# Norms of a decoder step: variance, root and reciprocal taken for five columns, and two tiles centred from PSUM

## What is computed

```python
sh, sc, g = mods[:, :, 0], mods[:, :, 1], mods[:, :, 2]
f = _swiglu(x * (1.0 + sc) + sh, w_ffn_in[l, 0], w_ffn_out[l, 0])
x = _layernorm(DEEPNORM_ALPHA * x + 0.5 * g * f, ln_g[l, 0], ln_b[l, 0])

def _layernorm(x, g, b):
    mu = jnp.mean(x, axis=-1, keepdims=True)
    var = jnp.mean(jnp.square(x - mu), axis=-1, keepdims=True)
    return (x - mu) * lax.rsqrt(var + LN_EPS) * g + b
```

## Time and profile before

| | us |
|---|---|
| median of three runs | 2399.42 |
| the three runs | 2395.73, 2399.42, 2406.4 |
| the profiled execution's own time | 2399.58 |
| its span, first to last instruction | 2397.8 |
| PE busy | 2275.1 (95%) |
| ACT, DVE, POOL busy | 726.8, 846.7, 904.9 |
| mean granted clock of TensorE | 0.968 of full |

### The profile page before, as it was taken

The page is one execution under the profiler, slowest core; times in us unless marked ns, Lnnn a source line. Parts: engine busy times, 40 slices in busy tenths (PEclk is TensorE's granted clock), DMA queues, the critical chain, the costliest instruction groups (busy, mean ns, idle before and its releaser), DMA issues.

```text
span 2397.8 us, 44766 instructions
## 1 busy us (share of the span) xinstructions
PE 2275.1 (95%) x18650; PEld 2127.4 (89%) x18650; DVE 846.7 (35%) x1001; ACT 726.8 (30%) x1049; POOL 904.9 (38%) x473
## 2 busy tenths in 40 slices
PE   7999999989998798999999999999999989999996
PEld 5999988869984388999999899998889979999995
DVE  1222213226768554222124422212343463222133
ACT  4222222252234325222222522222242225222223
POOL 2344432334420235444434444432344444444442
PEclk8999999989999998999999999999999989999998
DMA  9232376626746421323553232366623322233331
GB/s 309 81 95 87 97 236 190 207 87 195 217 130 197 143 86 55 95 87 95 188 174 98 62 96 88 89 203 195 208 89 96 89 72 71 87 94 90 103 88 48
DMA packets 455586, 300.60 MB, mean 125 GB/s; under 512 B 20446, under 2 KB 435006, under 8 KB 455350
## 3 DMA queue, kind: packets, MB, share of 16 engines
q1 hardware_dynamic: 455478, 299.04, 41.0%
HBM read 293.45 MB, written 5.55 MB: 125 GB/s over the span
## 4 chain that ended last, share of the span: by engine, by line
PE 80%; issue 7%; DVE 4%; POOL 4%; SPq 2%; ACT 1%; DMA 1%; POOLq 0%; DVEq 0%; ACTq 0%
PE ps L822 71%; PE ps L845 2%; POOL x L490 2%; POOL w_lo L759 2%; PE ps L884 1%; DVE sq L1833 1%; PE ps L835 1%; SPq L556 1%; SPq L551 1%; POOL samp_t L503 1%; DMA ada_w<-w_ada 1%; PE ps L898 1%; DVE x L1813 1%; DMA ada_first<-w_ada 0%; DVE h_lo L1799 0%
## 5 line engine op out<-in xcount | busy, mean ns | idle before, releaser
L759 POOL TENSOR_TENSOR w_lo<-raw,w_hi 128x1024 fp32r<-128x1024 f32 (+1 forms) x303 | 791.7, 2613 | 1230.5 <-ACT w_hi L1441 1230.3
L822 PE MATMUL ps<-h_hi,w_hi 128*128 128x260 f32 x3584 | 726.7, 284 | 15.1 <-DVE h_lo L2102 8.9
L822 PE MATMUL ps<-h_hi,w_lo 128*128 128x260 f32 x3584 | 724.5, 284 | 0.0
L822 PE MATMUL ps<-h_lo,w_hi 128*128 128x260 f32 x3584 | 723.7, 284 | 0.0
L1441 ACT ACTIVATE w_hi<-raw 128x1024 fp32r<-128x1024 f32 (+1 forms) x303 | 341.3, 1127 | 1159.4 <-PE ps L822 1089.6
L822 PEld LDWEIGHTS ps<-h_hi,w_hi 128*128 128x128 f32 x3584 | 555.3, 189 | 22.1 <-DVE h_lo L2102 9.3
L822 PEld LDWEIGHTS ps<-h_hi,w_lo 128*128 128x128 f32 x3584 | 555.1, 189 | 0.0
L822 PEld LDWEIGHTS ps<-h_lo,w_hi 128*128 128x128 f32 x3584 | 553.7, 189 | 0.0
L822 PE MATMUL ps<-hid_hi,w_hi 128*128 128x260 f32 x1408 | 294.5, 290 | 0.0
L2169 DVE TENSOR_TENSOR gated<-silu_a,ps 128x520 f32<-128x520 f32 x88 | 61.3, 697 | 656.8 <-PE ps L822 638.2
L822 PE MATMUL ps<-hid_hi,w_lo 128*128 128x260 f32 x1408 | 283.9, 283 | 0.0
(11 more groups left out here) (294 smaller groups left out, 1719.1 us busy)
## 6 DMA issues: line engine op xcount, KB each, us to landing
raw<-w_ffn_in SPq DMA_DIRECT2D x173, 512.0 KB, 3.6
ada_w<-w_ada SPq DMA_DIRECT2D x120, 512.0 KB, 6.3
raw<-w_ffn_out SPq DMA_DIRECT2D x64, 704.0 KB, 4.5
pages<-cache_k SPq DMA_DIRECT2D x64, 256.0 KB, 3.3
pages<-cache_v SPq DMA_DIRECT2D x64, 256.0 KB, 3.4
raw<-w_in_even SPq DMA_DIRECT2D x27, 512.0 KB, 5.3
raw<-w_in_odd SPq DMA_DIRECT2D x23, 512.0 KB, 3.6
ada_first<-w_ada SPq DMA_DIRECT2D x10, 1024.0 KB, 11.9
```

The costliest lines, as they stand in the source:

```text
L759: pool.tensor_tensor(w_lo[:, k, 0:kt, :], raw[:, k, 0:kt, :], w_hi[:, k, 0:kt, :].bitcast(F32), ALU.subtract).then_inc(chunk_cut, chunks)
L822: mm = pe.matmul(ps[:, 2 * q + half, 0:HT], w[:, k, t, :], v[:, kt0 + t, half, :], start=start and t == 0 and step == 0, stop=stop and t = ...
```

## The change

PE no longer makes the variance as a 128x520 tile. `column_sums` uses 128 tokens of the sums of squares as the weights and one column of `mean_w` as the moving operand; the result is one column with the tokens along the partitions. Four blocks of 128 tokens and a fifth that ends with the last token (overlapping the fourth) make five columns for the mean square, from two parts each, and five for the difference of mean and `shift`: 15 matmuls. ACT squares five columns, DVE subtracts, ACT takes the root, DVE the reciprocal, all on 128x5. Then each column is multiplied into the identity, which gives diagonal blocks (three on DVE, two on ACT, the last of them eight columns wide), and two matmuls with a block of ones spread the values over all partitions, into `pair(2)`, from which DVE normalises as before.

DVE centres two tiles, and takes the mean from PSUM for them; POOL centres the others. In the norms with conditioning groups, PE does one group, then waits for the blocks and spreads them, then does the other three; ACT stores the sums of all four groups behind its own blocks.

```diff
-CENTRE = 1
+CENTRE = 2
+TOKENS_AT = (0, 128, 256, 384, NTOK - 128)
...
-            eng.tensor_tensor(x[:, t], x[:, t], mean[:, :, :], ALU.subtract).then_inc(centred[part], 1)
+            eng.tensor_tensor(x[:, t], x[:, t], mean[:, :, :] if part else pair(2), ALU.subtract).then_inc(centred[part], 1)
...
+            def column_sums(bank, *parts):
+
+                for j, at in enumerate(TOKENS_AT):
+                    for v in parts:
+                        mm = pe.matmul(ps[:, bank, j:j + 1], v.rearrange("p h c -> p (h c)")[:, at:at + 128], mean_w[:, 0:1],
+                                       start=v is parts[0], stop=v is parts[-1])
+                return mm
+
+            def spread_rdev(n):
+
+                pe.wait_ge(spread_made, len(TOKENS_AT) * (n + 1))
+                for half in range(2):
+                    mm = pe.matmul(ps[:, 4 + half, 0:HT], ones, spread[:, half, :], start=True, stop=True)
+                mm.then_inc(rdev_done, 1)
...
-                pe.wait_ge(sq_added, (KT - 2) * (n + 1))
-                for half in range(2):
-                    pe.matmul(ps[:, half, 0:HT], mean_w, sq_sum[:, half, :], start=True, stop=False)
                 pe.wait_ge(samp_added, KT * (n + 1))
...
                 pe.wait_ge(squared, KT * (n + 1))
-                for half in range(2):
-                    mm = pe.matmul(ps[:, half, 0:HT], mean_w, sq[:, (KT - 1) % 2, half, :], start=False, stop=True)
-                mm.then_inc(var_done, 1)
+                pe.wait_ge(sq_added, (KT - 2) * (n + 1))
+                column_sums(1, sq_sum[:, :, :], sq[:, (KT - 1) % 2])
+                pe.wait_ge(delta_steps, 5 * n + 1)
+                column_sums(0, shift[:, :, :]).then_inc(var_done, 1)
                 for i in after:
                     group(n, i)
                     if i > after[0]:
                         turn_group(n, i - 1)
+                    else:
+                        spread_rdev(n)
+                if not after:
+                    spread_rdev(n)
...
-                act.wait_ge(delta_steps, 3 * n + 1)
-                act.activation(shift[:, :, :], shift[:, :, :], ACT.Square).then_inc(delta_steps, 1)
-                if ADAS[n]:
-                    group_sums(n, after_groups(n)[0])
-                act.wait_ge(delta_steps, 3 * n + 3)
+                act.wait_ge(var_done, n + 1)
+                act.activation(delta_sq, ps[:, 0, 0:5], ACT.Square, scale=D / 128).then_inc(delta_steps, 1)
+                act.wait_ge(delta_steps, 5 * n + 3)
                 act.wait_ge(eps_ready, 2)
-                act.activation(dev, dev, ACT.Sqrt, bias=eps_ln[:, :]).then_inc(dev_done, 1)
-                for i in after_groups(n)[1:]:
+                act.activation(dev, dev, ACT.Sqrt, bias=eps_ln[:, :]).then_inc(delta_steps, 1)
+                act.wait_ge(delta_steps, 5 * n + 5)
+                for j, at, of in ((3, 384, ident), (4, 512, ident[:, 120:128])):
+                    act.activation(spread_flat[:, at:at + of.shape[1]], of, ACT.Identity, scale=rdev[:, j:j + 1]).then_inc(spread_made, 1)
+                for i in after_groups(n):
                     group_sums(n, i)
...
                 dve.tensor_tensor(shift[:, :, :], pair(2), shift[:, :, :], ALU.subtract).then_inc(delta_steps, 1)
-                dve.wait_ge(delta_steps, d0 + 2)
-                dve.wait_ge(var_done, n + 1)
-                dve.tensor_tensor(dev, pair(0), shift[:, :, :], ALU.subtract).then_inc(delta_steps, 1)
                 centre(dve, n, 0)
-                dve.wait_ge(dev_done, n + 1)
-                dve.reciprocal(pair(2), dev).then_inc(rdev_done, 1)
+                dve.wait_ge(delta_steps, 5 * n + 2)
+                dve.tensor_tensor(dev, ps[:, 1, 0:5], delta_sq, ALU.subtract).then_inc(delta_steps, 1)
+                dve.wait_ge(delta_steps, 5 * n + 4)
+                dve.reciprocal(rdev, dev).then_inc(delta_steps, 1)
+                dve.wait_ge(delta_steps, 5 * n + 5)
+                for j in range(3):
+                    dve.tensor_scalar(spread_flat[:, 128 * j:128 * j + 128], ident, rdev[:, j:j + 1], None, ALU.mult
+                                      ).then_inc(spread_made, 1)
                 dve.wait_ge(rdev_done, n + 1)
```

More of the change, by code:

```diff
@@ L225, in build_step @@
         sq = put("sq", [128, 2, 2, HT], F32, R_TMP + 12 * NTOK)
-        dev = sq[:, 0]
+        spread = sq[:, 0]
+        spread_flat = spread.rearrange("p h c -> p (h c)")
+        norm_cols = put("norm_cols", [128, 3, 8], F32, R_TMP + 4 * NTOK)
+        delta_sq, dev, rdev = (norm_cols[:, u, 0:5] for u in range(3))
         res = new("res", [128, 1710])
@@ L369, in build_step @@
         var_done = sem("var_done")
-        dev_done = sem("dev_done")
+        spread_made = sem("spread_made")
         rdev_done = sem("rdev_done")
@@ L1862, in norm @@
             def norm(n):
-                d0 = 3 * n
                 dve.wait_ge(mean_ready, n + 1)
                 dve.tensor_tensor(shift[:, :, :], pair(2), shift[:, :, :], ALU.subtract).then_inc(delta_steps, 1)
-                dve.wait_ge(delta_steps, d0 + 2)
-                dve.wait_ge(var_done, n + 1)
-                dve.tensor_tensor(dev, pair(0), shift[:, :, :], ALU.subtract).then_inc(delta_steps, 1)
                 centre(dve, n, 0)
-                dve.wait_ge(dev_done, n + 1)
-                dve.reciprocal(pair(2), dev).then_inc(rdev_done, 1)
+                dve.wait_ge(delta_steps, 5 * n + 2)
[6 more added lines that the diff above has]
+                                      ).then_inc(spread_made, 1)
                 dve.wait_ge(rdev_done, n + 1)
```

## The result

The changed kernel takes 2427.07 us (median of four runs, 2424.36 to 2432.04) against 2400.27 for the kernel before (four runs, 2395.73 to 2406.4): ratio 1.0112, interval 1.0084 to 1.0141, 27 us slower. The direction is that of the forecast, the size is not: the time lies above the upper end of the range, 2422. The profiled execution took 2428.48, its span is 2426.7 (2397.8 before), and the mean granted clock is 0.961 of full (0.968).

The account below looks back on a forecast made before the run. PE, busy for 95% of the span, was taken as the bound, so only its waits for six norms could change. 3 x 3.35 + 2 x 0.3 + 1.8 = 12.45 us on 2399.58 gave 2412.0; range 2399.5 to 2422.

Parts of the forecast that it names:

- the mean: In each of six norms, the mean's matmul goes first, so ACT's whole 0.72 us wait for it goes.
- columns and small steps: In each norm, fifteen column matmuls take 3.7 us (bounds 1.6 and 6.7); square, subtraction, root and reciprocal take 0.9.
- The two tiles from PSUM: DVE's centring of two tiles in a norm costs 1.30 us, hidden under PE's columns.
- the step on which the forecast hung: The spread: DVE's blocks wait behind POOL's centrings, so PE has its go at 7.4 us; bounds 5.5 and 6.4.
- C: Rival, chance 0.12: not slower; POOL does not hold the blocks, PE is called at 5.5 us; total 2399.6.
- B: Rival, chance 0.20: DVE keeps its turn, three blocks go one behind another, ready at 6.4 us; +5.4, total 2405.
- A: The forecast itself, chance 0.52: 2412 us, 12.45 us added over the six norms.
- my zero: The end of ACT's last square in a norm, from which the prediction counts all times.
- The sign that was named for being wrong: The forecast is wrong if the last group is stored before the first normalised tile, or the clock there reads 0.5.
- The groups, moved: Norms 0, 2 and 3: three groups behind the spread delay ACT's scaling from 8.69 to 13.15 us; net +3.35 each.
- Back to normalising: Spread takes 1.04 us, normalising starts at 8.6, 0.75 later; +0.3 in norms 1 and 4, +1.8 in the last.
- D: Rival, chance 0.12: PE's clock falls in the norms with groups; +3.6 us in three norms on top of A, 2423.

Follow-up runs that it names:

- wide_filled: The changed kernel with 96 columns moved per column sum and five 260-column matmuls on PE ahead of its wait for the blocks: 2414.3 us, ratio 1.0062.
- wide_hold_filled: The changed kernel with 96 columns per column sum, POOL waiting until the blocks are made, and two 260-column matmuls in PE's wait: 2403.46 us, ratio 1.0012.
- after: The changed kernel itself, against the kernel before: 2427.07 us, ratio 1.0112.
- wide: The changed kernel with 96 equal columns moved instead of one in each column sum: 2425.25 us, ratio 1.0100 to the kernel before.
- wide_hold: The changed kernel with 96 columns per column sum and POOL waiting ahead of its fourth centring until the blocks are made: 2404.25 us, ratio 1.0021.
- hold: The changed kernel with POOL waiting ahead of its fourth centring until the diagonal blocks are made: 2412.5 us, ratio 1.0057 to the kernel before.
- groups_first: The changed kernel with all four groups on PE ahead of the spread: 2432.2 us, ratio 1.0142 to the kernel before.
- moved_groups: The kernel before with only PE's groups two to four behind the reciprocal and ACT's stores behind the root: 2416.88 us, ratio 1.0067.

## Why the prediction was right and where it was wrong

**Right: the mean.** 0.72 for each norm was taken back; of 4.3 us of waiting 0.8 is left, in norm 1.

**Right: columns and small steps.** 3.7 us were taken, 30 records took 3.50 (476.38 to 479.88) at the upper level, in norms 0 and the last. Where the clock fell among them they took 4.0 to 4.7, and 6.4 in norm 1, within the bound of 6.7. For square to reciprocal 0.9 was taken, 1.0 measured. The two tiles from PSUM took 1.29 (1.30) under the columns.

**Right: the step on which the forecast hung.** POOL's waiting centring goes first, then a block of DVE, in turn: the spread was called at 7.15 (7.4 forecast). In norm 0 the first block ended 0.1 behind POOL's fourth centring, the second 0.1 behind its fifth. In the last norm, where POOL has one tile more, the blocks took 3.57 and normalising began at 10.3 (9.65). C falls, for POOL did hold the blocks: with POOL held back they took 0.28 each. B falls, for a second block waited too in norms 0, 2, 4 and the last, and the spread came at 7.15 and not at 6.4. In norm 1 the blocks began at 7.9, when POOL was through, and took 0.28 each as well. The Trainium skill (SBUF — State Buffer, the section on the two separate sides) describes an exclusive lock on a port pair that DVE and GpSimd share; these runs agree with it, by the 1316 ns against 288.

**Right: the sum of A at the upper clock.** A's figures can be held against wide_filled, where the clock stays: +3.1, +3.5 and +3.1 in the norms with groups (forecast +3.35 each), +0.3 and +0.6 in norms 1 and 4 (+0.3), +2.2 in the last (+1.8): 12.7 against 12.45. In norms 1 and 4 that is partly luck: the spread was called at 8.3, not 7.4, because the columns began at the lower level, but the kernel before was behind my zero there too, its mean having waited 1.4 and 1.2 us and not 0.72. By the runs it is +14.9, interval 9.8 to 20.2. And C's figure, 2399.6 if nothing holds the blocks, can be held against wide_hold_filled: 2403.46, or +2.9 with an interval of -0.5 to +6.2. Taking POOL out of the way is worth the difference of the two, 12.0 us (5.8 to 18.2).

**Wrong: the clock stood in a rival of its own.** The sign that was named for being wrong came: the clock read 0.5. The step that failed is "The groups, moved": it took the second group's start to the last store, 4.5 us, from a stretch in which PE was never idle, and "Back to normalising" took the spread's 1.04 likewise. Measured in norm 2, at the lower level, they were 8.0 us (1332.75 to 1340.77) and 2.10. The change takes away just that condition: three of the four groups no longer run while the chain goes on, and PE waits. D said so, priced it at +3.6 in three norms on top of A, and got 0.12; but D was no alternative to A, it followed from it. Only if the spread is late does PE wait long, so with A likely D was likely too. Measured, after less wide_filled, by norms: +1.7, +4.3 and +4.5 in norms 0, 2 and 3, +1.3 in norm 1, -0.2 in norm 4, +1.0 in the last: 12.8 us, of which D's three norms are 10.6 (its price was 10.8). That the sum fits is partly luck: in norm 0 the clock came back before the third group, and in norms 2 and 3 the spread was slow beside the groups, which D had not counted. By the two ratios it is 12.0, with their intervals taken together 3.4 to 20.6. A plus D is 2423; norms 1, 4 and the last, outside D's figure, add 2.1, which is 2425. The last 2 us to the median lie within the spread of its four runs. The range ended at 2422, short of A plus D, and so left out the time.

**Not foreseen: columns that cost the clock themselves.** I read the earlier trace rows for what a column matmul costs at either level and not for what it does to the level. In after the clock fell among them in norms 2, 3 and 4. wide, wide_hold and the two filled kernels show no fall among the columns of norms 0, 2, 3 and the last, 16 norms in all; the fall in wide's norm 2 came later, in the wait. Norms 1 and 4 say the same from the other side. The clock is low there as the norm begins, in the kernel before too, except in norm 4 of after and of wide_hold. With one column it stayed low for 17.7 us and more after the square, in all five such norms of after, hold and groups_first, though PE was busy throughout the columns (5.60 of 5.60 us in norm 1 of after). With 96 columns it rose among them, 4.0 to 4.6 us after the square, in all seven.

The Trainium skill (TensorE: Matmul & The Clock Gate, Part 1) says that the gate is set by how busy PE has been recently. PE's wait in moved_groups agrees with that (0.50 at the end of 5.32 us of idling). The columns do not, if busy is what the profile's busy time shows: 1.40 of 1.40 us in hold and 5.60 of 5.60 in after, at 0.50. Which part of PE's work counts is not settled by these runs.

**What stays of the loss without clock and POOL.** wide_hold_filled still needs 1.3 to 1.8 us more than before in each norm with groups, close to the 1.45 that C had for the moved groups. There PE has 3.6 us of columns, 1.0 of spread and the groups in its queue, where it had 1.0 for the variance; the shorter chain on ACT and DVE (6.6 to normalising instead of 7.8) waits for the last group's store. That follows from the timelines; no run took the column sums off PE. Norms 1 and 4, where C had -1.6 each, gave 0.0 and +0.4: the clock was low as their columns began, and the spread was called at 7.5 and 7.7. In norm 4 of wide_hold, where it was at 1.00 from the start, the spread was called at 5.4 and the norm took 1.8 us less than before. By that one norm, part of what is left is still the clock.

## What to carry to other kernels

Work that fills PE's waits is not only hidden, it can hold TensorE at 2.4 GHz for what comes behind, as the extra matmuls of wide_filled did in the two norms where wide had lost it: before moving such work, look up the granted clock of the stretch and price everything up to the next long stretch of matmuls at both levels, as a consequence of the wait and not as a case beside it. DVE's blocks between SBUF tiles took 0.28 us with POOL idle and up to 1.32 with POOL's operations queued beside them; here a wait ahead of one POOL operation brought 13 us. And a big change is best taken apart: its two smallest parts were the ones that did not cost time.

## What the runs showed that was not expected

- TensorE at 0.50 while PE was busy in 1.40 of 1.40 us with 128x128 weights and one moving column; with 96 moving columns 30 such records took 3.6 us, at 1.00.
- The level at which a norm runs is not the same from norm to norm in one execution: wide, three norms with the same steps at the same offsets, kept the clock in two and lost it in one. The four runs of that kernel spread over 14 us, those of wide_filled over 6.5; that this comes from the clock is not shown, and the ten runs of wide_hold spread over 14 us too.
- In hold a spread called 1.7 us earlier (5.48 instead of 7.15 in norm 0) saved 2.9 us there; the stretch at the lower level shrank with it, from 6.9 us to 3.4.
